# The tenth expert weight piece moves into two rooms outside the ring, and the embeddings' loads move behind it

## The reference, cut to what matters

```python
h = rmsnorm(x, g_mix[i]); proj = h @ w_in[i]
...
x = x + mixed @ w_out[i]
x = x + moe_swiglu(rmsnorm(x, g_ffn[i]), w_router[i], b_router[i],
                   w_up[i], b_up[i], w_down[i], b_down[i])
...
# in moe_swiglu, for every expert e:
gu = xb @ w_up[e] + b_up[e]                      # 1024 x 2048 weights
g = jnp.minimum(gu[:, :D_FF], SWIGLU_LIMIT)
up = jnp.clip(gu[:, D_FF:], -SWIGLU_LIMIT, SWIGLU_LIMIT)
act = (up + 1.0) * g * jax.nn.sigmoid(SWIGLU_ALPHA * g)
y = act @ w_down[e] + b_down[e]                  # 1024 x 1024 weights
...
ple_gate = jax.nn.sigmoid(rmsnorm(x, g_ple_gate[i]) @ w_ple_gate[i])
ple = rmsnorm(p[i] @ w_ple_proj[i], g_ple_post[i])
x = x + ple_gate * ple
```

## Time and profile before

| what | value |
|---|---|
| median of 3 runs | 1169.3 us (1168.94 to 1169.32) |
| span of the profiled execution, first to last instruction | 1167.7 us, the execution as a whole not timed apart |
| granted TensorE clock, mean | 0.989 |
| PE busy | 1119.7 us (96%) |
| DVE, ACT, POOL busy | 386.6, 177.3, 157.7 us |
| data moved | 441.04 MB, mean 378 GB/s |

### The profile page before, as it was taken

One profiled execution on the slowest core, in us unless ns is written; L12 is line 12 of the kernel. 1 busy time (PEld: TensorE's weight loads), 2 busy tenths in 40 slices (PEclk: granted clock), 3 DMA queues, 4 the chain that ended last, 5 costly groups with the idle time before them and its releaser, 6 DMA issues.

```text
span 1167.7 us, 15793 instructions
## 1 busy us (share of the span) xinstructions
PE 1119.7 (96%) x6530; PEld 499.1 (43%) x6530; DVE 386.6 (33%) x823; ACT 177.3 (15%) x304; POOL 157.7 (14%) x167
## 2 busy tenths in 40 slices
PE   8999999999999999999999999999999999999998
PEld 4588787533333433333333333333333333333344
DVE  6546859442222222222232222222222222222226
ACT  2262012420000000000211101101011010101113
POOL 2995655300000000000000000000000000000005
PEclk9999999999999999999999999999999999999999
DMA  9932437799999999999999999999999999999991
GB/s 314 336 132 73 145 141 291 316 414 427 427 429 433 427 434 431 429 434 432 427 434 431 428 435 432 428 434 431 428 434 432 428 434 432 428 435 426 427 416 44
DMA packets 40047, 441.04 MB, mean 378 GB/s; under 512 B 9748, under 2 KB 10064, under 8 KB 22352
## 3 DMA queue, kind: packets, MB, share of 16 engines
q1 hardware_dynamic: 38800, 436.91, 89.0%
q0 software_dynamic: 1104, 3.67, 0.9%
q10 hardware_dynamic: 112, 0.02, 0.0%
HBM read 439.54 MB, written 1.05 MB: 377 GB/s over the span
## 4 chain that ended last, share of the span: by engine, by line
PE 62%; DMA 36%; DVE 1%; issue 1%; ACT 0%; SPq 0%; DVEq 0%
DMA ring<-in_w_up_dram 20%; PE bank L1788 20%; DMA ring<-in_w_down_dram 15%; PE bank L1843 12%; PE bank L1468 7%; PE bank L1483 4%; PE bank L1860 3%; PE bank L1628 2%; PE bank L1636 2%; PE bank L1762 2%; PE bank L1664 2%; PE bank L1965 1%; PE bank L1826 1%; PE bank L1542 1%; PE bank L1897 1%
## 5 line engine op out<-in xcount | busy, mean ns | idle before, releaser
L1788 PE MATMUL bank<-ring,arena 128*64 128x512 f32 x2048 | 454.5, 600 | 17.3 <-DMA ring<-in_w_up_dram 17.2
L1788 PEld LDWEIGHTS bank<-ring,arena 128*64 128x64 f32 x2048 | 144.4, 138 | 322.1 <-issue 290.2
L1843 PE MATMUL bank<-ring,arena 128*64 128x512 f32 x1024 | 233.5, 610 | 16.5 <-DMA ring<-in_w_down_dram 14.5
L1266 DVE TENSOR_TENSOR arena<-arena,bank 128x512 f32<-128x512 f32 x128 | 79.5, 682 | 291.0 <-PE bank L1860 290.9
L1843 PEld LDWEIGHTS bank<-ring,arena 128*64 128x64 f32 x1024 | 74.7, 140 | 154.7 <-issue 145.7
L1242 DVE TENSOR_SCALAR arena<-bank 128x512 f32<-128x512 f32 x32 | 22.1, 691 | 351.8 <-PE bank L1788 351.8
L631 POOL TENSOR_TENSOR ring<-ring 128x2048 f32<-128x2048 f32 x1 | 4.5, 4534 | 904.0 <-DMA ring<-in_w_ple_gate_dram 904.0
L819 ACT ACTIVATE arena<-arena 128x512 f32<-128x512 f32 x32 | 20.2, 630 | 494.3 <-DVE arena L1242 494.3
L1468 PE MATMUL bank<-arena,ring 128*128 128x256 f32 x384 | 86.4, 383 | 0.0
L1468 PEld LDWEIGHTS bank<-arena,ring 128*128 128x128 f32 x384 | 71.9, 190 | 12.6 <-issue 3.5
L1860 PE MATMUL bank<-arena 64*128 64x512 f32 x256 | 63.5, 615 | 0.0
(11 more groups left out here) (279 smaller groups left out, 794.7 us busy)
## 6 DMA issues: line engine op xcount, KB each, us to landing
ring<-in_w_up_dram SPq DMA_DIRECT2D x40, 4096.0 KB, 33.3
ring<-in_w_down_dram SPq DMA_DIRECT2D x24, 4096.0 KB, 34.9
ring<-in_w_up_dram SPq DMA_DIRECT2D x45, 2048.0 KB, 23.5
ring<-in_w_down_dram SPq DMA_DIRECT2D x15, 2048.0 KB, 16.1
ring<-in_w_in_dram SPq DMA_DIRECT2D x7, 2048.0 KB, 14.9
ring<-in_w_up_dram SPq DMA_DIRECT2D x6, 1024.0 KB, 32.3
ring<-in_w_glu_dram SPq DMA_DIRECT2D x2, 2048.0 KB, 8.2
ring<-in_w_out_dram SPq DMA_DIRECT2D x2, 2048.0 KB, 7.6
```

The lines of the kernel that those rows point to most:

```text
L1266: dve.tensor_tensor(part, part, bank[at][:, :], ALU.add).then_inc(m["sc_add"], 1)
L1788: last = pe.matmul(bank[UG + w][HALF * h:HALF * (h + 1), :].rearrange("p (m j) -> p m j", j=4), XS[:, k, :], columns[:, h, :, :], start=Fa ...
L1843: last = pe.matmul(bank[YB][HALF * c:HALF * (c + 1), :], ACTT[:, j, HALF * h:HALF * (h + 1)], piece[:, j, 512 * c:512 * (c + 1)], start=(h ...
```

## The change

Piece `(1, 3)` no longer goes through the ring. Its first half (the even rows, 1 MB) is loaded to the area at `A_BT` when `out4` is full, its second half to the area at `A_X` when `lg1` is full, both from SP's queue between piece 8 and the wait for `head_read`, each with a semaphore of its own (`extra_in_0`, `extra_in_1`). TensorE reads it from there. Piece 10, `(1, 4)`, now goes into place 0 in two halves on the waits that piece 9 had, and all later pieces have their place shifted by one: `spot` is (i - 1) modulo 9 from there on. Pieces 11 to 18 wait for piece i - 10, and from 19 on for i - 9 as before. POOL's seven loads wait until TensorE has read piece `(1, 3)` (`READ[3]` at 2), since they go into the same two areas. Since the places are shifted, other pieces lie side by side: expert 4's down pieces are issued as a pair (`PAIRED`), and in the loop the single pieces are the first two of the first expert of three, where they were the third and fourth of the second.

```diff
+        EXTRA = (1, 3)
+        PAIRED = (4, 4)
+        AHEAD = PLACES
         def spot(n, c):
-            return (PER_EXPERT * n + c) % PLACES
+            i = PER_EXPERT * n + c
+            if isinstance(n, int) and i > AHEAD:
+                i -= 1
+            return i % PLACES
-        HALVES = {(1, 3): "early_half", (E - 2, 3): "late_0", (E - 1, 3): "late_1", (E - 1, 5): "late_2"}
+        HALVES = {(1, 4): "early_half", (E - 2, 3): "late_0", (E - 1, 3): "late_1", (E - 1, 5): "late_2"}
...
+        EXTRA_ROWS = (area(A_BT, 2 * F), area(A_X, 2 * F))
...
                 load_rows(at, expert_source(i // PER_EXPERT, i % PER_EXPERT))
+            for k, job in enumerate(("out4", "lg1")):
+                wait_full(sp, job)
+                sp.dma_start(EXTRA_ROWS[k], expert_source(*EXTRA)[:, 2 * F * k:2 * F * (k + 1)]).then_inc(S[f"extra_in_{k}"], 16)
             def left(n, c):
-                if c < 3:
+                if isinstance(n, int) and PER_EXPERT * n + c <= 2 * AHEAD:
+                    before, piece = divmod(PER_EXPERT * n + c - AHEAD - 1, PER_EXPERT)
+                    sp.wait_ge(READ[piece], before + 1)
+                elif c < 3:
                     sp.wait_ge(READ[c + 3], n - 1)
                 else:
                     sp.wait_ge(READ[c - 3], n)
...
-                if isinstance(n, int) and (n, c) == (1, 3):
+                if isinstance(n, int) and (n, c) == (1, 4):
                     sp.wait_ge(S["head_read"], 1)
...
-            wait_full(pool, "lg1")
+            pool.wait_ge(READ[EXTRA[1]], EXTRA[0] + 1)
             pool.dma_start(WPP, w_ple_proj[0].rearrange("(k p) n -> p k n", p=P)).then_inc(S["ple_in"], 16)
-            wait_full(pool, "out4")
             pool.dma_start(PIN, p[0, 0].rearrange("(t p) n -> p t n", p=P)).then_inc(S["ple_in"], 16)
...
                     for k in (2 * c, 2 * c + 1):
+                        if aside:
+                            pe.wait_ge(S[f"extra_in_{k % 2}"], 16)
```

More of the change, by code:

```diff
@@ L243, in hybrid_layer @@
                  "down_bias_in gain_in gate_gain_in cast_set cast_first_set rest_set_0 rest_set_1 up_bias_in up_bias_set post_in ple_in pp_ms pp_root "
-                 "pt_full pt_set pp_full pp_set gt_full gt_set bias_full bias_add head_read early_half late_0 late_1 late_2 xt3_late xt3_again xt3_again_set gate_set gw_sum gm_sum gp_full gp_read pg_sum x3_set x3_sq x3_ms x3_root xt3_full xt3_set pg_full "
+                 "pt_full pt_set pp_full pp_set gt_full gt_set bias_full bias_add head_read extra_in_0 extra_in_1 early_half late_0 late_1 late_2 xt3_late xt3_again xt3_again_set gate_set gw_sum gm_sum gp_full gp_read pg_sum x3_set x3_sq x3_ms x3_root xt3_full xt3_set pg_full "
                  "pg_sig fin_set stored dve_step act_step pool_step").split()
@@ L282, in loads @@
                 for c in range(PER_EXPERT if n < E else 2):
+                    if (n, c) == EXTRA:
+                        continue
                     if not (n < E and c % 2 and together(n, c - 1)):
@@ L285, in loads @@
                         last[n, c] = count[spot(n, c)]
-                    elif n < FIRST + PERIOD:
+                    elif n < FIRST + PERIOD and (n, c - 1) != PAIRED:
                         count[spot(n, c - 1)] += 1
@@ L509, in load_pair @@
                     load_piece(n, like, c + 1)
-            for i in range(PLACES, PER_EXPERT * FIRST):
+            for i in range(AHEAD + 1, PER_EXPERT * FIRST):
                 n, c = divmod(i, PER_EXPERT)
@@ L515, in _ @@
                 for c in range(PER_EXPERT):
+                    if (n, c) == PAIRED:
+                        load_pair(n, n, c)
+                    if PAIRED in ((n, c), (n, c - 1)):
+                        continue
                     left(n, c)
@@ L1780, in up @@
                         pe.wait_ge(S[HALVES[n, c]], 16)
-                    piece = chunk(spot(n, c) if halves else piece_in(c), c)
+                    aside = isinstance(n, int) and (n, c) == EXTRA
+                    if not aside:
+                        piece = chunk(spot(n, c) if halves else piece_in(c), c)
                     for k in (2 * c, 2 * c + 1):
+                        if aside:
+                            pe.wait_ge(S[f"extra_in_{k % 2}"], 16)
                         if halves and k == 2 * c + 1:
                             piece_in(c)
+                        row = EXTRA_ROWS[k % 2] if aside else piece[:, k % 2, :]
                         for w in range(2):
                             for h in range(2):
-                                columns = piece[:, k % 2, F * w:F * (w + 1)].rearrange("p (m h j) -> p h m j", h=2, j=4)
+                                columns = row[:, F * w:F * (w + 1)].rearrange("p (m h j) -> p h m j", h=2, j=4)
                                 last = pe.matmul(bank[UG + w][HALF * h:HALF * (h + 1), :].rearrange("p (m j) -> p m j", j=4),
```

## The result

The changed kernel takes 1170.89 us (median of 19 runs, 1170.28 to 1172.37), the kernel before beside it 1168.92 us (19 runs, 1168.23 to 1169.39): a ratio of 1.0018, with a 95% interval of 1.0012 to 1.0024. Forecast were 1168.6 us, 0.7 us gained; measured are 2.0 us lost. The time lies in the whole range and just inside the 0.2% that the forecast calls no change, but above the range of the forecast case itself (1167.5 to 1170.1), and the sign is wrong, which the forecast named as what would refute it. The profiled execution took 1171.5 us with a span of 1169.7.

What follows compares the result with a forecast made beforehand. The DMA weight stream was taken to bound the kernel: 1.8 us from the restart plus 4.87 for one piece gave 6.7 ahead, less 6.0 for the moved loads, 0.7 gained, so 1168.6 us, range 1165.8 to 1171.7.

Steps and rivals of the forecast that it cites:

- the whole range: Total time from 1165.8 to 1171.7 us, leaving out the whole-piece rival (0.12) and the change not done (0.03).
- the forecast case itself: Total time 1168.6 us, 0.7 us gained, own range 1167.5 to 1170.1; chance 0.76.
- The bound: Whole kernel: the experts end when the weight stream ends, so only an earlier landing of the last weight piece gains time.
- The early load: Before expert 0: two 1 MB halves land in the idle hole at 230.6 and 233.0 us, at no cost.
- The order of waits: Around 273 us: one ring issue falls away, POOL's loads start just there and fill the slot, leaving no gap.
- The clock term: Near expert 29: a wait may lower TensorE's clock; 1.7 us lost less 1.1 of slack would cost 0.6 us.
- the price of the moved loads: At about 275 us: POOL's seven loads, 2.10 MB, delay every later piece by 6.04 us; bounds 4.9 and 9.0.
- The rival of the braked stream: From 273 to 300 us: POOL's packets slow the ring's; loads cost 9.0 us against 6.7, giving 1171.6 us; chance 0.09.
- the restart: After the hole before expert 0: the stream finds free engines, so the piece issued at 239.74 lands 1.8 us earlier, at 246.9.
- the bound of 5.8: At the restart: low bound of the stream's lead, if 0.9 us of excess belongs to the restart, not the embeddings; otherwise 6.7.
- the dry slot: Near 280 us: without the moved loads, the slot lacking an issue would run dry, losing 0.5 us.
- The sum: Whole kernel: 6.7 us of stream lead less 6.0 for the moved loads, 0.7 gained; between 1.8 gained and 0.2 lost.

Runs made afterwards that it cites:

- the other runs: Changed kernel with the seven loads left out (1165.61 us), in SP's queue (1170.72), at expert 8 (1172.31); kernel before with only POOL's loads moved (1175.97).
- the two runs with 7.2 and 7.3 us: Kernel before with only POOL's loads moved, 1175.97 us; changed kernel with piece 10 loaded whole instead of in halves, 1171.42 us.

## Why the prediction was wrong

**Right**, by its own steps. The bound: the end still follows the stream, and 2.4 us late at 300 us are 1.8 us late at the last expert (L1868 starts at 1128.52, L1843 before at 1126.70). The other 0.6 the kernel before loses for itself in its profiled execution at 322 us, where two of its landings lie 5.5 us apart. The early load: landings at 230.7 and 233.6, forecast 230.6 and 233.0, and they cost nothing. The order of waits: POOL's issues at 273.6 to 277.6 stand where the slot falls away, and 277 to 284 us run at 423 GB/s. The clock term: the granted clock falls to 0.58 over 4 us behind the wait of 2.30 us at 1063.94, and 32 matmuls take 8.79 us; 1.7 us lost, and TensorE still waits 0.34 us for the last down weights, so here the slack covered all of it.

**Wrong: the price of the moved loads**, 6.04 us against 7.8 in the changed kernel's trace (6.9 to 7.4 by the other runs). The step took the engine time of these transfers with an empty ring's queue beside them. That leaves out what they do to others. Without `b_down` the trace shows a price of 5.3 us for 1.84 MB, 1.0 more than their 4.3 us of bytes, about the excess that 6.04 has over 4.9. The rest is the brake: four loads of 0.26 MB cost 2.5. The rival of the braked stream was given 0.09. Its mechanism was right in that the ring's packets are slowed while POOL's pass, and its time of 1171.6 is 0.7 from the measured; its price came from another row (9.0 us, at 234 GB/s) and it had the whole 2.10 MB brake, where it is one eighth of them. That row, 234 to 235 us, lies just where the four `b_down` loads land (234.7 to 235.5), so it may have been theirs; no run shows it. The evidence that was held against it, 408 GB/s from 230.5 to 234, was of a time in which nothing else was there to be braked.

**Wrong: the restart**, 1.8 us against 0.4 to 0.5. The step let the second half land 2.43 us behind the first, at 240.9 (it lands 3.9 behind, at 242.5), let the piece issued at 239.74 land as if alone and then spaced all later ones by 4.87 us. In the changed kernel that landing comes 1.4 us late (8.6 against 7.2), in the two runs with 7.2 and 7.3 us the next one does, 1.4 and 1.1 us (6.3 and 6.0 apart, not 4.9). The 0.9 us of excess that the earlier trace rows show before belonged to the restart, the case that the bound of 5.8 allowed for, and the measured lead of 5.4 lies below even that.

**Wrong, without effect: the dry slot**, 0.5 us against 1.9 in the trace without the loads. In the changed kernel the moved loads cover it.

The sum was 6.7 - 6.0 = 0.7 gained. Measured it is 5.4 - 7.8 = 2.4 lost at 300 us, 2.0 at the end. Either error alone would have turned the sign: 6.7 - 7.8 and 5.4 - 6.0 are both losses. Of the 3.1 us between the two sums the brake of the `b_down` loads explains most of the first 1.8; why the restart lost its 1.3 stays open. That the time still lies in the range owes nothing to the sum: the range reached up to 1171.7 for the braked stream, to which the forecast gave 0.09.

## What to carry to other kernels

A transfer's own engine time, read where it runs alone, can be too low for what it costs inside a full stream (here 6.0 against 6.9 to 7.8 us). Ask which partitions it writes: here a few small loads into 32 or 64 partitions braked the big ones beside them, where the same bytes over all 128 hardly did, and a load over partitions 32 to 95 did not. To bring a piece forward and push others back in the same saturated stream is a trade of bytes for bytes, and it pays only if what comes in costs less per byte than what it displaces. Behind a hole, a first piece that lands early is a gain only if the next one does too.

## What the runs showed of the hardware that was not expected

- 256 KB into 32 or 64 partitions at a time cost 2.5 to 2.8 us in a stream of 430 GB/s, the same bytes over 128 partitions 0.9. 128 KB into partitions 32 to 95 left the stream at 428 GB/s, into 0 to 63 at 405. The time is the same from either queue (1170.9 and 1170.7 us).
- Behind an idle stretch of the DMA engines 1.1 to 1.4 us are lost within the first two or three transfers, beyond the 2.3 us by which a lone piece takes longer than its bytes, in halves or whole. With the dip between them filled, the 4 us behind it run at 348 GB/s instead. The cause is open.
- A slot that runs dry in mid-stream, by the forecast's arithmetic for half a us, costs 1.9 us in the trace without the moved loads. The cause is open.
